# In-products of two FFNs and of a short convolution by one level of Strassen, down-products in a phase of their own

## The chip, the cores and the metric

One core of one Trainium2 chip. The metric is the device time of the whole program in microseconds: 2456.89 us, median of 3 runs (2454.88 to 2457.57).

## The reference, cut to what matters

Two layers on 1024 tokens of width 1024 (plus 256 context tokens in the first). The change touches what follows the attention and recurrence mixer of layer 0: an FFN, the short convolution mixer of layer 1, and the FFN of layer 1. FFN_HIDDEN is 2816; everything is float32.

```python
def swiglu(h, w_gu, w_down):
    gt, up = jnp.split(h @ w_gu, 2, axis=-1)
    return (jax.nn.silu(gt) * up) @ w_down

def short_conv_mixer(h, w_in, w_conv, w_out):
    bg, cg, xv = jnp.split(h @ w_in, 3, axis=-1)
    return (bg * dwconv(cg * xv, w_conv, SC_PAD)) @ w_out
...
    h = h + g1 * y            # y: the mixer of the layer
    h = h + g2 * swiglu(modulate(rmsnorm(h, norm2_g[l]), sh2, sc2), ffn_w_gu[l], ffn_w_down[l])
...
return rmsnorm(h, final_g)
```

## The kernel before, in words

**Layout.** Features lie on the 128 partitions, tokens along the row: h is [128, 8, 1024]. A float32 product is made of three fp32r matmuls of 128x512 (`product`, L795): high weight by high token, low weight by high token, high weight by low token. So each operand is first split into a high part (rounded to fp32r) and a low part (the rest), for weights by GpSimd (`split`, L622: L628 high, L631 low), for tokens by ScalarE (high) and VectorE (low).

**Memory.** The tensors made by `keep` (L114 to L140) lie at the front of each partition's memory in the order in which they are made: act_hi 0 to 32 KB, act_lo 32 to 64, w_hi4 64 to 80, w_lo4 80 to 96, raw, small ones. `at(kb, ...)` (L85) places a tensor at kb kilobytes behind what is kept at that moment, and lets others overlap it: the calls ahead of `act_hi` therefore lie over the kept tensors themselves (x_rms over act_hi), and those from L143 on lie behind all kept ones (h, w_hi2 at 32, hid_hi and z_hi at 64, o_hi at 68 and 81, o_lo at 91).

**Stages.** (1) norms, projections, gates and recurrence; (2) attention; (3) its output projection (`project_out`, 16 groups of 24 matmuls); (4) FFN 0: 11 rounds over 256 hidden columns each. A round is `gate_up` (L1109) for two tiles and two halves of 512 tokens (8 groups of 8 x 3 matmuls), then 16 down groups of 2 x 3 matmuls (half, output tile m), each added into h by VectorE (`update`, L1683). (5) Short convolution: 4 rounds of 12 groups of 24, a width-3 convolution along the tokens on VectorE (`short_conv`, L2089: L2094, L2096), then 16 down groups. (6) FFN 1 as FFN 0. (7) the final norm: transposes, squares, scaled rows, stores. During the first six rounds of FFN 0 VectorE also sums the modulation vectors of layer 1 (`mod_unit`, L1691: 6 vectors of 8 units of 128x1024).

**Order.** Every engine runs its own written-out list in order and waits on semaphores. SP issues nearly all loads in order: a weight unit of 512 KB into one of two raw buffers when the unit two before is split (`load_unit`, L405). TensorE's results go through 8 PSUM banks. The last round of a stage is arranged so that the half-0 norm of the next stage is made while half-1 groups run (`last_norms`, L1326 on ScalarE, L1743 on VectorE; `norm_sum` and `norm_spread` on TensorE, L814 and L821). A norm: squares (ScalarE), sums (VectorE), a sum over partitions (TensorE), root (ScalarE), inverse and diagonal (VectorE), spread (TensorE), scale (VectorE, L1665), shift (ScalarE, L1309, an Identity with bias), low part (VectorE).

## Time and profile before

| what | value |
|---|---|
| median of 3 runs | 2456.89 us (2454.88 to 2457.57) |
| profiled execution, span from first to last instruction | 2456.4 us; no other time of this execution is recorded, and the span lies within the runs |
| granted TensorE clock over the span | 0.996 |
| TensorE matmul busy | 2413.7 us (98%), 11158 matmuls |
| VectorE, GpSimd, ScalarE busy | 1115.1 (45%), 1053.0 (43%), 512.9 us (21%) |
| DMA | 207.08 MB, mean 84 GB/s |

Busy time is the union of the spans of an engine's instructions. A matmul's span (390 ns) overlaps that of the next, so what one costs is read from start to start. Idle time of an engine that isn't the bottleneck costs nothing.

### The profile page before, as it was taken

How to read it: one execution, taken by the hardware profiler on the slowest of the kernel's cores; microseconds unless marked ns; L12 is line 12 of the kernel's file. 1: busy time of each engine (PE TensorE's matmuls, PEld its weight loads, DVE VectorE, ACT ScalarE, POOL GpSimd, SP SyncE). 2: the span in 40 equal slices, each digit the busy share in tenths (PEclk: the TensorE clock that was granted, in tenths of full speed). 3: DMA queues.
4: the chain of work that ended last, by engine and by line, in shares of the span. 5: the costliest groups of instructions: out<-in, count | busy, mean ns of one | idle time of the engine just before them, and what ended most of it. 6: DMA issues, size and time to landing. Idle time of an engine off the chain costs nothing.

```text
span 2456.4 us, 29288 instructions
## 1 busy us (share of the span) xinstructions
PE 2413.7 (98%) x11158; PEld 1981.8 (81%) x11158; DVE 1115.1 (45%) x1427; ACT 512.9 (21%) x816; POOL 1053.0 (43%) x507
## 2 busy tenths in 40 slices
PE   8999999989999999999999999999999999999998
PEld 3888878878888888888888888887888888888887
DVE  5677858853734444422224634246522222222224
ACT  4544438851200000000002200002200000000003
POOL 3333347888633334443343243443444433333440
PEclk9999999999999999999999999999999999999999
DMA  9444465523432333211111111111211111111111
GB/s 304 155 145 156 152 164 106 105 104 104 128 116 98 104 120 120 86 43 43 51 51 37 42 44 51 51 52 43 61 52 51 43 44 48 45 43 51 51 43 69
DMA packets 223343, 207.08 MB, mean 84 GB/s; under 512 B 40135, under 2 KB 193443, under 8 KB 222755
## 3 DMA queue, kind: packets, MB, share of 16 engines
q1 hardware_dynamic: 216787, 187.16, 26.0%
q10 hardware_dynamic: 5904, 16.78, 2.0%
q0 software_dynamic: 576, 2.10, 0.2%
q8 instruction: 51, 0.84, 0.1%
q14 instruction: 25, 0.20, 0.0%
HBM read 185.73 MB, written 20.28 MB: 84 GB/s over the span
## 4 chain that ended last, share of the span: by engine, by line
PE 93%; DVE 3%; ACT 1%; issue 1%; POOL 0%; DMA 0%; SPq 0%; DVEq 0%; POOLq 0%; ACTq 0%
PE bank L798 29%; PE bank L800 29%; PE bank L799 29%; PE bank L911 1%; DVE probs L1978 1%; PE bank L1041 1%; PE bank L1067 1%; PE bank L1066 1%; PE bank L1028 1%; PE bank L832 1%; ACT probs L1504 1%; PE bank L1029 1%; DMA mod_ring<-in_mod_w 0%; DVE bank L1649 0%; DVE bank L1665 0%
## 5 line engine op out<-in xcount | busy, mean ns | idle before, releaser
L628 POOL TENSOR_TENSOR w_hi<-raw,ones 128x1024 fp32r<-128x1024 f32 x184 | 359.1, 1952 | 1176.4 <-PE bank L800 1123.0
L798 PE MATMUL bank<-act_hi,w_hi 128*128 128x512 f32 x2160 | 843.2, 390 | 2.7 <-DVE act_lo L1844 2.7
L799 PE MATMUL bank<-act_hi,w_lo 128*128 128x512 f32 x2168 | 845.5, 390 | 0.0
L800 PE MATMUL bank<-act_lo,w_hi 128*128 128x512 f32 x2160 | 841.9, 390 | 0.0
L798 PEld LDWEIGHTS bank<-act_hi,w_hi 128*128 128x128 f32 x2160 | 406.1, 188 | 87.1 <-issue 2.8
L799 PEld LDWEIGHTS bank<-act_hi,w_lo 128*128 128x128 f32 x2168 | 408.2, 188 | 84.5
L631 POOL TENSOR_TENSOR w_lo<-raw,w_hi 128x1024 fp32r<-128x1024 f32 x184 | 469.3, 2550 | 14.4
L800 PEld LDWEIGHTS bank<-act_lo,w_hi 128*128 128x128 f32 x2160 | 406.0, 188 | 85.1
L1688 DVE SCALAR_TENSOR_TENSOR h<-bank,mods,h 128x512 f32<-128x512 f32 x432 | 318.9, 748 | 243.5 <-PE bank L800 242.8
L2028 DVE TENSOR_TENSOR hid_f<-silu_g,bank 128x512 f32<-128x512 f32 x86 | 59.1, 687 | 677.9 <-PE bank L800 675.6
L798 PE MATMUL bank<-hid_hi,w_hi 128*128 128x512 f32 x704 | 275.9, 392 | 0.8 <-DVE hid_lo L2035 0.8
L799 PE MATMUL bank<-hid_hi,w_lo 128*128 128x512 f32 x704 | 274.3, 390 | 0.0
L800 PE MATMUL bank<-hid_lo,w_hi 128*128 128x512 f32 x704 | 274.3, 390 | 0.0
L1564 ACT ACTIVATE silu_g<-bank 128x512 f32<-128x512 f32 x88 | 52.6, 598 | 774.9 <-PE bank L800 774.9
L798 PEld LDWEIGHTS bank<-hid_hi,w_hi 128*128 128x128 f32 x704 | 132.2, 188 | 30.8 <-DVE h L1688 2.1
L800 PEld LDWEIGHTS bank<-hid_lo,w_hi 128*128 128x128 f32 x704 | 132.2, 188 | 28.0
L799 PEld LDWEIGHTS bank<-hid_hi,w_lo 128*128 128x128 f32 x704 | 132.2, 188 | 27.1
L1570 ACT CAST hid_hi<-hid_f 128x512 fp32r<-128x512 f32 x86 | 53.4, 621 | 460.7 <-DVE hid_f L2028 460.7
L2035 DVE TENSOR_TENSOR hid_lo<-hid_f,hid_hi 128x512 fp32r<-128x512 f32 x86 | 78.5, 913 | 59.1 <-ACT hid_hi L1570 59.1
L1699 DVE SCALAR_TENSOR_TENSOR mod_acc_f<-mod_in_f,cond,mod_acc_f 128x1024 f32<-128x1024 f32 x42 | 65.3, 1556 | 13.8 <-DMA mod_in_f<-in_mod_w 13.2
L2086 DVE TENSOR_TENSOR t_pad<-cg_sb,bank 128x512 f32<-128x512 f32 x16 | 11.0, 690 | 129.3 <-PE bank L800 129.2
L1504 ACT ACTIVATE probs<-probs,low_all 128x768 f32<-128x768 f32 (+1 forms) x64 | 63.5, 993 | 26.6 <-DVE low_all L1978 26.1
(232 smaller groups left out, 2331.0 us busy)
## 6 DMA issues: line engine op xcount, KB each, us to landing
raw<-in_ffn_w_gu SPq DMA_DIRECT2D x88, 512.0 KB, 3.8
mod_in_f<-in_mod_w SPq DMA_DIRECT2D x48, 512.0 KB, 4.5
raw<-in_ffn_w_down SPq DMA_DIRECT2D x44, 512.0 KB, 3.6
mod_in_p<-in_mod_w SPq DMA_DIRECT2D x32, 512.0 KB, 6.5
raw<-in_o_w_in SPq DMA_DIRECT2D x24, 512.0 KB, 3.7
raw<-in_e_w_in SPq DMA_DIRECT2D x20, 512.0 KB, 5.0
mod_ring<-in_mod_w SPq DMA_DIRECT2D x16, 512.0 KB, 9.0
raw<-in_e_w_out SPq DMA_DIRECT2D x16, 512.0 KB, 3.7
```

Source lines behind the costliest of these rows:

```text
L628: nc.gpsimd.tensor_tensor(w_hi, raw[:, parity, :], ones[:, 0:1].to_broadcast([P, UNIT]), ALU.mult).then_inc(s_hi, 1)
L631: nc.gpsimd.tensor_tensor(w_lo, raw[:, parity, :], w_hi, ALU.subtract).then_inc(s_split, 1)
L798: pe.matmul(dst, w_hi, x_hi, start=first, stop=False)
L799: pe.matmul(dst, w_lo, x_hi, start=False, stop=False)
L800: return pe.matmul(dst, w_hi, x_lo, start=False, stop=last)
L1504: nc.scalar.activation(probs[s % 3][:, 0:w], probs[s % 3][:, 0:w], ACT.Exp, bias=low_all[:, s:s + 1], scale=-1.0, accum_out=sums[:, s:s + ...
L1564: nc.scalar.activation(silu_g[:, q % 2, :], bank[:, b, :], ACT.Silu).then_inc(s_silu, 1)
L1570: nc.scalar.copy(hid_hi[:, tile, half * HALF:(half + 1) * HALF], from_).then_inc(s_hidh, 1)
L1688: V.scalar_tensor_tensor(out=dst, in0=bank[:, b, :], scalar=mods[:, gate, m:m + 1], in1=dst, op0=ALU.mult, op1=ALU.add).then_inc(s_hup, 1)
L1699: ins = V.scalar_tensor_tensor(out=acc[:], in0=ring[:, k % 2, :], scalar=cond[:, k, 0:1], in1=acc[:], op0=ALU.mult, op1=ALU.add)
L2028: V.tensor_tensor(hidden_from(i, q), silu_g[:, q % 2, :], bank[:, b, :], ALU.mult).then_inc(s_hidf, 1)
L2035: V.tensor_tensor(hid_lo[:, tile, sl], hidden_from(i, q), hid_hi[:, tile, sl], ALU.subtract).then_inc(s_hid, 1)
```

## The change

**In-products.** Take a pair of 128-column weight units A and B (for the FFNs gate tile and up tile; for the convolution two units of w_in), the two halves of the 8 feature tiles (k 0 to 3, k 4 to 7) and the two halves of the tokens. This 2x2x2 block product took eight half products of 4 x 3 matmuls; it is now made by seven (the Winograd form of Strassen): products 0 and 3 use plain tokens (a11, a12), products 1, 2, 4, 5 and 6 sums or the second half of the tokens, and weights or sums of weights. VectorE makes four weight sums a pair and seven combinations of the products from PSUM (U2, U3, U4, C11, C12, C21, C22). Pairs: 22 for each FFN, 12 for the convolution (8 that give c * x and are convolved, 4 "gated").

**Weight operands.** Each of the seven has one slot (128x512, high and low) that is filled when its product of the pair before is done: high part by ScalarE (before: GpSimd), low part by GpSimd. The two raw units are loaded once the low part of product 5 and of product 6 of the pair before is made.

**First products.** Products 0 and 3 of the first four pairs need only the first half of the tokens; these eight run first, while the norm and the sums of the second half are made.

**Down phase.** The gated rows z (silu x up, or gated convolution) go to DRAM (z_spill). After all pairs, chunks of 128 rows of z and of the down weight are loaded, split (ScalarE high, GpSimd low) into four slots, and multiplied two chunks a round; the last two rounds are one with four chunks.

**The rest.** The modulation sums of layer 1 run in halves of 128x512 in pairs 4 to 15 of FFN 0. All loops (Fori) are unrolled. In the diff the first seven tensors are declared ahead of act_hi, so over the kept tensors, the next six behind them. Diff, cut to its core:

```diff
+        low_f = at(32, "low_f", [P, FT, SEQ])
+        a22 = at(64, "a22", [P, 4, SEQ], F32R)
+        p1 = at(80, "p1", [P, 4, HALF])
+        silu_g = at(88, "silu_g", [P, 2, HALF])
+        mod_acc_f = at(92, "mod_acc_f", [P, UNIT])
+        conv_t = at(88, "conv_t", [P, 2, SEQ])
+        a21 = at(88, "a21", [P, 4, HALF])
...
+        a11 = at(32, "a11", [P, 2, 4, HALF], F32R)
+        a12 = at(48, "a12", [P, 2, 4, HALF], F32R)
+        slot_hi = at(64, "slot_hi", [P, 7, HALF], F32R)
+        slot_lo = at(78, "slot_lo", [P, 7, HALF], F32R)
+        t_sum = at(92, "t_sum", [P, 2, HALF])
+        t_pad = at(96, "t_pad", [P, SEQ + 2])
...
+        EARLY = 4
+        FIRST = ((0, 0), (0, 1), (3, 0), (0, 2), (3, 1), (0, 3), (3, 2), (3, 3))
+        REST = (1, 2, 4, 5, 6)
+        ACTS = {
+            0: [(a11[:, HI, k, :], a11[:, LO, k, :]) for k in range(4)],
+            1: [(act_lo[:, k, one], act_lo[:, k, two]) for k in range(4)],
+            2: [(act_lo[:, 4 + k, one], act_lo[:, 4 + k, two]) for k in range(4)],
+            3: [(a12[:, HI, k, :], a12[:, LO, k, :]) for k in range(4)],
+            4: [(act_hi[:, k, two], act_hi[:, k, one]) for k in range(4)],
+            5: [(act_hi[:, 4 + k, two], act_hi[:, 4 + k, one]) for k in range(4)],
+            6: [(a22[:, k // 2, k % 2 * HALF:(k % 2 + 1) * HALF], a22[:, 2 + k // 2, k % 2 * HALF:(k % 2 + 1) * HALF]) for k in range(4)],
+        }
...
@@ SP @@
+            def load_pair(st, p, b):
+                if p:
+                    sp.wait_ge(s_wlo, product_at(st, 5 if b else 6, p - 1) + 1)
...
+            def load_mod_half(h):
+                n, k, a = h // 16, h % 16 // 2, h % 2
+                if h >= 3:
+                    sp.wait_ge(s_macc, MACC + h - 2)
+                sp.dma_start(p1[:, 1 + h % 3, :], mod_w[1, n, k][:, a * HALF:(a + 1) * HALF]).then_inc(s_mp[h % 3], 16)
...
+                    if p:
+                        store_z(st, p - 1, 0)
+                    if p + 1 < PAIRS[st]:
+                        load_pair(st, p + 1, 1)
+                    if p:
+                        store_z(st, p - 1, 1)
+                    if p + 1 < PAIRS[st]:
+                        load_pair(st, p + 1, 0)
+                    if mods_here:
+                        for h in range(h0 + 3, min(h0 + 11, 16 * MODS)):
+                            load_mod_half(h)
...
+            def load_down(st, c):
+                r, last = c // 2, PAIRS[st] - 1
+                if r >= 2:
+                    sp.wait_ge(s_out, OUT[st] + 16 * (r - 1))
+                else:
+                    sp.wait_ge(s_prod, product_at(st, 5 if r else 2, last) + 1)
...
+            def load_hidden(st, c):
+                r, last = c // 2, PAIRS[st] - 1
+                if r >= 2:
+                    sp.wait_ge(s_out, OUT[st] + 16 * (r - 1))
+                else:
+                    sp.wait_ge(s_prod, product_at(st, 6 if r else 1, last) + 1)
+                stored_z(st, c)
...
@@ GpSimd @@
+            def down_low(st, c):
+                for j, (hi, lo, full) in enumerate((hid_slot(c), down_slot(c))):
+                    pool.wait_ge(s_h2, half_chunk(st, c) + j + 1)
+                    nc.gpsimd.tensor_tensor(lo, full, hi, ALU.subtract).then_inc(s_l2, 1)
...
+                operand_low(st, 4, 0)
+                operand_low(st, 5, 0)
+                for k in range(4):
+                    token_sum_low(st, 5, k)
+                operand_low(st, 6, 0)
+                for p in range(1, PAIRS[st]):
+                    for n in operands(st, p):
+                        operand_low(st, n, p)
...
@@ TensorE @@
+            def operand_product(st, n, p, bank_, ready=None):
+                at_, s = product_at(st, n, p), slot_at(n, p)
+                pe.wait_ge(s_wlo, at_ + 1)
+                for k in range(4):
+                    if ready is not None:
+                        pe.wait_ge(*ready(k))
+                    w = (slot_hi[:, s, k * P:(k + 1) * P], slot_lo[:, s, k * P:(k + 1) * P])
+                    mm = product(bank[:, bank_, :], w, *ACTS[n][k], k == 0, k == 3)
+                mm.then_inc(s_prod, 1)
...
+            def pair_products(st, p):
...
+                if every:
+                    pe.wait_ge(s_xfree, g)
+                    operand_product(st, 0, p, x_bank(p))
+                if g:
+                    pe.wait_ge(*made(g - 1, C22))
+                operand_product(st, 1, p, P5_BANK, ready.get(1))
...
+                if g:
+                    pe.wait_ge(*made(g - 1, C21))
+                operand_product(st, 2, p, P6_BANK, ready.get(2))
+                if every:
+                    pe.wait_ge(s_p1, g + 1)
+                    operand_product(st, 3, p, x_bank(p))
+                operand_product(st, 4, p, P7_BANK, ready.get(4))
+                operand_product(st, 5, p, P3_BANK, ready.get(5))
+                pe.wait_ge(*made(g, U2))
+                operand_product(st, 6, p, P4_BANK, ready.get(6))
...
+            def down_products(st):
+                last = ROUND[st] - 2
+                for r in range(last):
+                    for idx in range(16):
+                        down_group(st, r, idx, (2 * r, 2 * r + 1), DOWN_BANK[idx % 4], down_free(st, r, idx))
+                four = range(2 * last, 2 * last + 4)
+                for idx in range(8):
+                    down_group(st, last, idx, four, DOWN_BANK[idx % 4], down_free(st, last, idx))
...
@@ ScalarE, joint of two stages, from the norm of the second half on @@
+                first_product_copied(st, 0)
                 rms(n + 1)
+                first_product_copied(st, 1)
+                second_half(st, 0)
+                operand_high(st, *FIRST[7])
+                operand_high(st, 1, 0)
+                second_half(st, 1)
+                for m in (1, 2, 5):
+                    token_sum_high(st, m, 0)
+                second_half(st, 2)
+                operand_high(st, 2, 0)
+                for m in (1, 2, 5):
+                    token_sum_high(st, m, 1)
+                first_product_copied(st, 2)
+                second_half(st, 3)
+                for m in (1, 2, 5):
+                    token_sum_high(st, m, 2)
+                first_product_copied(st, 3)
...
@@ VectorE, a pair (mod_halves only in pairs 4 to 15 of FFN 0) @@
+                mod_halves(0, 2)
+                dve.wait_ge(s_prod, product_at(st, 3, p) + 1)
+                dve.wait_ge(s_p1, g + 1)
+                V.tensor_tensor(x, x, first, ALU.add).then_inc(s_made, 1)
+                dve.wait_ge(s_prod, product_at(st, 2, p) + 1)
+                V.tensor_tensor(first, p6, first, ALU.add).then_inc(s_made, 1)
...
+                    weight_sum(st, 1, ahead)
+                    weight_sum(st, 2, ahead)
+                mod_halves(2, 4)
+                dve.wait_ge(s_prod, product_at(st, 4, p) + 1)
+                V.tensor_tensor(first, p7, first, ALU.add).then_inc(s_made, 1)
...
```

Here product n of a pair is `operand_product(st, n, p, ...)`; `first` is the pair's copied product 0 in p1, `x` its X bank; s_prod counts products, s_wlo low parts of weight operands, s_out down groups, s_macc modulation halves.

## Rows read from the trace of the kernel before

**Rows 1.** The page, busy time of the engines and their share of the span

```profile
PE 2413.7 (98%) x11158; PEld 1981.8 (81%) x11158; DVE 1115.1 (45%) x1427; ACT 512.9 (21%) x816; POOL 1053.0 (43%) x507
```

**Rows 2.** Windows: us; PE, PEld, DVE, ACT, POOL busy (instructions); clock; DMA

```profile
690.00:1030.00 340.00, 340.00 (x1541) 282.05 (x1541) 142.12 (x168) 24.39 (x40) 135.27 (x60) 1.00 0.33 108
...
1300.00:1380.00 80.00, 78.61 (x359) 64.23 (x358) 44.42 (x72) 26.12 (x40) 18.69 (x9) 1.00 0.12 34
...
1660.00:1740.00 80.00, 78.44 (x357) 63.68 (x356) 54.23 (x80) 22.09 (x36) 30.59 (x14) 1.00 0.19 53
```

**Rows 3.** Waits of TensorE: total us, times, longest

```profile
PE bank L818 <- DVE sumsq L1649: 2.4, 3, 0.8
```

**Rows 4.** Timeline of TensorE, FFN 0: start us, us, what; first and last of 97

```profile
1099.65 0.39 PE L798 MATMUL bank<-act_hi,w_hi 128*128 128x512 f32 x1
...
1121.41 0.39 PE L798 MATMUL bank<-act_hi,w_hi 128*128 128x512 f32 x1
```

**Rows 5.** Timeline of VectorE, one round of FFN 0 apart

```profile
1172.68 0.69 DVE L2028 TENSOR_TENSOR hid_f<-silu_g,bank 128x512 f32<-128x512 f32 x1 [10.15 <-PE bank L800]
...
1238.03 0.69 DVE L2028 TENSOR_TENSOR hid_f<-silu_g,bank 128x512 f32<-128x512 f32 x1 [10.15 <-PE bank L800]
```

**Rows 6.** Timeline of TensorE, output projection; first and last of 16 matmuls

```profile
542.15 0.39 PE L798 MATMUL bank<-act_hi,o_hi 128*128 128x512 f32 x1
...
545.65 0.40 PE L798 MATMUL bank<-act_hi,o_hi 128*128 128x512 f32 x1
```

**Rows 7.** Timeline of VectorE, two down groups of the short convolution

```profile
1434.96 0.75 DVE L1688 SCALAR_TENSOR_TENSOR h<-bank,mods,h 128x512 f32<-128x512 f32 x1 [0.65 <-PE bank L800]
1436.36 0.75 DVE L1688 SCALAR_TENSOR_TENSOR h<-bank,mods,h 128x512 f32<-128x512 f32 x1 [0.65 <-PE bank L800]
```

**Rows 8.** Timeline of VectorE, a low part that met no GpSimd instruction

```profile
1174.06 0.69 DVE L2035 TENSOR_TENSOR hid_lo<-hid_f,hid_hi 128x512 fp32r<-128x512 f32 x1 [0.69 <-ACT hid_hi L1570]
```

**Rows 9.** Groups by form: xcount | busy us, mean ns | idle before

```profile
L631 POOL TENSOR_TENSOR w_lo<-raw,w_hi 128x1024 fp32r<-128x1024 f32 x184 | 469.3, 2550 | 14.4
...
L2035 DVE TENSOR_TENSOR hid_lo<-hid_f,hid_hi 128x512 fp32r<-128x512 f32 x86 | 78.5, 913 | 59.1 <-ACT hid_hi L1570 59.1
L1699 DVE SCALAR_TENSOR_TENSOR mod_acc_f<-mod_in_f,cond,mod_acc_f 128x1024 f32<-128x1024 f32 x42 | 65.3, 1556 | 13.8 <-DMA mod_in_f<-in_mod_w 13.2
...
L1570 ACT CAST hid_hi<-hid_f 128x512 fp32r<-128x512 f32 x86 | 53.4, 621 | 460.7 <-DVE hid_f L2028 460.7
...
L1309 ACT ACTIVATE act_hi<-bank,mods 128x512 fp32r<-128x512 f32 x48 | 32.8, 687 | 65.9 <-DVE bank L1665 65.7
...
L710 POOL TENSOR_TENSOR act_lo<-y_f,act_hi 64x512 fp32r<-64x512 f32 x16 | 20.5, 1283 | 16.5 <-ACT act_hi L1529 15.8
```

**Rows 10.** Timelines of VectorE and GpSimd, short convolution

```profile
1476.18 3.18 DVE L2096 SCALAR_TENSOR_TENSOR conv_t<-t_pad,par,conv_t 128x1024 f32<-128x1024 f32 x1 [0.15 <-DVE conv_t L2094]
1479.52 1.28 DVE L2096 SCALAR_TENSOR_TENSOR conv_t<-t_pad,par,conv_t 128x1024 f32<-128x1024 f32 x1 [0.15 <-DVE conv_t L2096]
...
1475.56 2.72 POOL L631 TENSOR_TENSOR w_lo<-raw,w_hi 128x1024 fp32r<-128x1024 f32 x1
```

**Rows 11.** DMA issues: xcount, KB each, median us to landing

```profile
raw<-in_ffn_w_down SPq DMA_DIRECT2D x44, 512.0 KB, 3.6
...
h<-h_spill SPq DMA_DIRECT2D x2, 1536.0 KB, 8.1
```

**Rows 12.** Timeline of ScalarE, a copy of 1024 columns

```profile
501.34 1.04 ACT L1539 CAST act_hi<-r_f 128x1024 fp32r<-128x1024 f32 x1
```

**Rows 13.** Windows around TensorE's longest gap; columns as in rows 2

```profile
531.20:534.40 3.20, 0.25 (x3) 0.10 (x1) 0.69 (x1) 0.58 (x1) 3.00 (x2) 1.00 0.60 172
534.40:541.20 6.80, 6.15 (x15) 4.80 (x16) 0.00 (x0) 0.62 (x1) 5.77 (x5) 0.50 0.27 77
```

**Rows 14.** Timeline of TensorE, sum and spread of a norm, end of FFN 0

```profile
1339.82 1.05 PE L818 MATMUL bank<-ones,sumsq 128*128 128x1 f32 x8 [0.78 <-DVE sumsq L1649]
...
1342.90 1.05 PE L825 MATMUL bank<-diag,ones 128*128 128x128 f32 x8
```

More of the change, by code:

```diff
@@ L218, in w_slot @@
         def w_slot(s):
-            return (w_hi4[:, s, :], w_lo4[:, s, :]) if s < 4 else (w_hi2[:, s - 4, :], w_lo2[:, s - 4, :])
+            return w_hi4[:, s, :], w_lo4[:, s, :]
         def out_slot(j):
@@ new lines, in x_bank, with p1_at, made, round_use @@
+        def x_bank(p):
+            return X_BANK[p] if p < EARLY else X_BANK[0]
+        def p1_at(p):
+            return p1[:, p if p < EARLY else 0, :]
+        C11, U2, U4, U3, C22, C12, C21 = range(1, 8)
+        def made(g, what):
+            return s_made, 7 * g + what
+        def round_use(st, r):
+            before = sum(len(range(r % 2, ROUND[k], 2)) for k in range(st))
+            return 32 * (before + r // 2 + 1)
+        def half_chunk(st, c):
+            return 4 * sum(ROUND[:st]) + 2 * c
@@ L1313, in norm_pair, with joint @@
+            def joint(st):
+                n, n0 = NORM[st], LAST_OUT[st]
+                if st != F0:
+                    for e in range(7):
+                        operand_high(st, *FIRST[e])
                 for f in range(FT):
```

1111 lines of the change are left out of this document (561 added, 550 removed).

## The prediction, made before the change was run

> **What bounds the kernel now.** I read the shares of the engines first: TensorE is busy in 98% of the span, no other engine in half of it [rows 1]. Then the stretches: from 690 to 1030 us TensorE is busy in all 340 us, and only the places where one stage hands over to the next show gaps, 1.4 and 1.6 us [rows 2]; its longest wait on the norms comes to 2.4 us in three waits [rows 3]. So the three stages that the change rewrites (FFN 0, short convolution, FFN 1) last as long as their matmuls do. Third, what a matmul costs: 96 steps from one 128x512 matmul to the next take 21.76 us, 0.2267 us each, although each row shows 0.39, since they overlap [rows 4]. An FFN round of 288 repeats after 65.35 us, 0.2269 each: changing groups costs nothing [rows 5].
>
> The step is not the same everywhere. Where the weights lie in o_hi and o_lo, 15 steps take 3.50 us, 0.2333 each [rows 6]; the short convolution's down groups of six take 1.40 us, again 0.2333 [rows 7]. Read with the allocation: in the fast rows weights and moving operand both lie among the kept tensors (act_hi, act_lo, w_hi4, w_lo4, the first 96 KB), or, for FFN down-products, both behind them (hid_hi, w_hi2). In both slow cases one lies in front and the other behind. I take that for the rule here.
>
> **The change part by part.**
>
> *Removed matmuls.* An in-product pair now (two column units, two token halves) is 2 x 2 x 8 x 3 = 96 matmuls; afterwards 7 x 4 x 3 = 84. There are 22 + 12 + 22 = 56 pairs: 672 fewer, at 0.2267: **-152.3 us**. The down-products keep their number.
>
> *Where the operands lie.* The new weight operands (slot_hi, slot_lo) lie behind the kept tensors. Products 0 and 3 move a11 and a12, also behind: fast. Products 1, 2, 4, 5, 6 move act_lo, act_hi and a22, all in front: slow. 56 x 5 x 12 = 3360 matmuls x 0.0067 = **+22.4**. The new down phase has both in front: fast, which gives back the three slow rounds of the short convolution, 288 x 0.0067 = **-1.9**. Bounds: no slow step at all (-22), all in-products slow (+9).
>
> *The steady pair* (from the fifth on) takes TensorE 24 x 0.2267 + 60 x 0.2333 = 19.4 us. DVE: 13 operations of which six read SBUF twice, 0.69 each where nothing blocks [rows 8] and about 0.6 from start to start: 9.3 with the gaps. GpSimd: seven low parts of 512 columns, 1.3 each (the 512-column row has 1.28 [rows 9]): 9.1. ScalarE: eight copies at 0.62 and two silus: 6. All are hidden. The tightest waits of TensorE: on C21 of the pair before, ready 0.8 us after that pair's end and wanted 5.5 after it; on the X bank, freed near 16 and wanted at 19.4. The weight loads of a pair are released by the low part of product 6, about 3.6 us into the pair before, and take 3.8; wanted at 13. Cost: 0.
>
> *The modulation sums* move into 12 pairs of FFN 0 as eight half units each, 0.65 per half (half of the unblocked 1.28 of conv_t, the same kind of step [rows 10]). DVE has 14.6 us of work there, in which 14 operations read SBUF twice and can meet GpSimd. That meeting has a price: a conv_t step that starts while GpSimd is at w_lo takes 3.18 us, the next one, alone, 1.28 [rows 10]; it waited for the whole instruction. On average it is less: hid_lo takes 0.913 [rows 9] for 0.69 alone [rows 8], so 0.22; mod_acc_f 1.556 for 1.28, 0.28. With 0.25 each: 14.6 + 3.5 = 18.1, and about 1 us for halves still landing (ring of three, each load issued on SP only when DVE has used the third before it, with z stores and weight loads queued behind these waits): 19.1 of 19.4. Just hidden; I take **+3** for all twelve, bounds 0 and 40.
>
> *The last down round of each stage.* The last two rounds become one over four chunks, so its first group needs all four. But the slots of the last two chunks are those of the round before, and their loads wait on SP for that round's end (s_out). From there: three loads of 512 KB are in after 5.7 us, four after 6.7 (one takes 3.6, 3 MB 8.1 [rows 11]: 1.8 us per further MB), the high copy 1.04 [rows 12], then four GpSimd low parts of 1024 columns at 2.55, one after the other: 9.3, 11.9, 14.4, 17.0. TensorE does nine of the group's twelve matmuls meanwhile (2.0) and stands otherwise. A gap of 3.9 us did more than cost itself: the granted clock fell to 0.50 (1.2 GHz) 3.2 us after the last matmul and stayed there for 6.8 us [rows 13]; of the loss of 3.4 I take 2.7. So 17.0 - 2.0 + 2.7 = 17.7 us, three times: **+53**, bounds 45 and 63. In other rounds the same chain of 17.0 has the 21.8 us of a round: hidden.
>
> *The joints.* Before the second half's operands exist TensorE has eight first products (21.8 us). ScalarE then has, after the spread of the norm (7.4 us in: two products, sum 0.9, spread 1.1; from the sum's start to the spread's 3.1 [rows 14]) and one scale (0.75), twelve Identity steps at 0.69 and fourteen copies at 0.62 before the fourth first product leaves its bank: at 25.1, while TensorE wants it at 21.0. 4.1, with gaps 4.5. Next, the loads of pair 1 wait for the low part of product 6 of pair 0, behind nine GpSimd instructions (11.7): issued 37.4, landed 41.2, summed, copied and split 43.9 to 45; TensorE comes at 41.8: about 3. Sum near 8 a joint, x 3 = **+24**, bounds 12 and 45, less the gaps of today's joints, 1.5 each [rows 2]: **-4.4**.
>
> *The start of the down phase.* Chunks 0 and 1 load when products 1 and 2 of the last pair are done; four low parts in a row end about 2 us after the last product. x 3: **+6**, bounds 0 and 18. *The first four pairs of the short convolution* have 14.0 us each for 9.3 + 3 conv_t steps (4.6 with their meetings): short by a little: **+3**, bounds 0 and 8. *z to DRAM and back*: stores of 0.5 MB a pair, loads long after; 0. *Unrolled instead of loops*: the attention and projection stages are unrolled already and keep 0.227 a step; 0, bounds -2 and 10. The tail has the same transposes and rows: 0, plus or minus 2.
>
> Sum: -152.3 + 22.4 - 1.9 + 3 + 53 + 24 - 4.4 + 6 + 3 = -47 us. The profiled execution has a span of 2456.4 us, 0.5 below the median of the runs (2456.9), so the two are one: **2410 us**.
>
> *A rule beside the rows.* The rows show two matmul steps by where the operands lie [rows 4, 6, 7]. The Trainium skill says otherwise (SBUF, Who interferes with whom: TensorE and ScalarE never wait on anyone; only the port pair of VectorE and GpSimd contends); by it every step would be 0.2267. Rows 6 and 7 speak against it for this case.
>
> **The rivals.**
> 1. *One matmul step for all.* The slow steps come from something else in those stretches and don't follow the operands. Without the 22.4: 2388 us. For it: the addresses stand in no row. Against: o_hi and w_hi rows 4 us apart, with the same moving operand, differ. Chance 0.14.
> 2. *The last rounds' operands are in time*, or the joints are covered better than I count: without the 53, 2357 us. Against: the wait is written in load_hidden and load_down. 0.07.
> 3. *Many small waits*: in-order queues (SP behind DVE's half units; ScalarE copying weights behind silus) cost 0.5 us in each of the 56 pairs: +28, 2438 us. For it: seven single-buffered operand slots and one raw pair. Against: several us of slack in each wait that I followed. 0.15.
> 4. *VectorE becomes the bound: slower.* Place: the 12 modulation pairs and the sum pairs of the short convolution, where it meets GpSimd. Price: with w us of wait per twice-reading operation, 12 x (14.6 + 14 w - 19.4); at w = 0.64 this eats the 47 us, and at 0.8 it gives 77, and the eight later sum pairs 7 more: 2491 us. For it: rows 10, and GpSimd never pauses long now. Against: 0.22 and 0.28 on average, and GpSimd's pieces are half as long. 0.10. The Trainium skill has this rule (SBUF, Two separate sides: of a VectorE operation with two SBUF inputs and a GpSimd one, the second to start blocks fully), and by the rule, the trace agrees in rows 10; it would give w up to 1.3 us and some 2610 us.
> 5. *The products are not fewer*: excluded by the counts in the code; 0.01.
>
> **How the numbers follow.** The forecast, 2395 to 2430, gets 0.53. A measurement of this kernel can tell about 0.2% (4.9 us) from no change. Faster: the forecast, rivals 1 and 2, and 0.13 of 3: 0.87; same 0.02 (the top of 3); slower 0.11 (4 and 5). The range takes in rival 1 below and 3 above: 2378 to 2450 us, and leaves out rivals 2 and 4.
>
> **What would show it.** Right: 4704 in-product matmuls; steps of 0.2333 in products 1, 2, 4, 5, 6 and 0.2267 in 0, 3 and the down phase; three gaps of TensorE near 10 and 4 us, ended by GpSimd's low parts, with the clock at 0.50 after them; gaps of 2 to 3 us ended by ScalarE's copies in the joints; pairs 19.4 us apart. Wrong: modulation pairs longer than 20 us with TensorE waiting for VectorE (rival 4), gaps inside every pair (rival 3), or no gap before the last round.

## The result, and the profile after

| kernel | median of the runs, us | against before, 95% interval |
|---|---|---|
| before | 2457.1 (2454.9 to 2457.6) | |
| changed | 2516.3 (2514.7 to 2518.1) | 1.0242 [1.0227, 1.0256] |

The change makes the kernel slower by 59 us; the forecast was 47 us faster. The forecast of 2410 misses by 106 us, and the measurement lies 66 us above the range.

The page of the changed kernel, busy time of the engines and the granted clock in forty slices, to be read beside [rows 1]:

```profile
PE 2351.8 (94%) x10486; PEld 1897.2 (75%) x10486; DVE 1553.6 (62%) x1963; ACT 840.4 (33%) x1327; POOL 1271.6 (51%) x735
...
PEclk9999999999998889899998999998999999999999
```

TensorE executes 672 matmuls fewer, as counted, but is busy only 62 us less instead of 152, and the span holds 162 us in which it is idle (43 before). Part of the busy time went into steps at half clock: of the 6 slices (62.8 us each) below 9, 4 lie between 750 and 1070 us, where the modulation sums run. The waits of TensorE from 535 us on (total us, times, longest); before there were 2.4 us on the norms [rows 3]:

```profile
PE bank L990 <- POOL act_lo L951: 37.6, 7, 11.5
PE bank L1025 <- DVE mod_acc_f L1833: 26.1, 6, 4.4
PE bank L990 <- ACT silu_g L1468: 16.0, 8, 3.2
PE bank L990 <- POOL act_hi L951: 14.8, 2, 11.8
PE bank L990 <- DVE act_hi L1896: 11.9, 6, 3.3
PE bank L990 <- ACT p L1460: 6.8, 3, 2.3
PE bank L990 <- DVE t_pad L1993: 6.8, 2, 6.5
```

The first and fourth line (52 us) are the last down rounds and the starts of the down phases, the fifth and sixth the joints (a joint is the change from one stage to the next): foreseen. The second is a wait that no step of the prediction has: `mod_totals` (L1025), 16 short matmuls of 128x1 that add a finished modulation sum over the partitions, stands in TensorE's order behind product 1 of every second modulation pair and waits for the last halves of the pair before. The windows (columns as in [rows 2]) place the loss: the modulation pairs, a steady stretch of FFN 1, one of the six half-clock stretches behind the totals, and the last round of FFN 0:

```profile
756.00:1062.00 306.00, 266.80 (x1052) 214.44 (x1051) 205.64 (x247) 69.16 (x120) 134.30 (x84) 0.88 0.43 131
1900.00:2200.00 300.00, 300.00 (x1293) 242.12 (x1292) 155.28 (x202) 91.32 (x157) 169.97 (x110) 1.00 0.26 80
771.40:778.20 6.80, 6.58 (x24) 5.91 (x25) 1.05 (x3) 0.00 (x0) 0.00 (x0) 0.50 0.73 228
1358.50:1375.60 17.10, 6.92 (x16) 4.96 (x17) 0.75 (x1) 8.25 (x12) 14.62 (x9) 0.50 0.30 92
```

The steady stretch is as predicted: no wait, 1293 matmuls in 300 us, 84 in 19.5 us. Of the 1052 matmuls of the first row 96 are the short ones of the totals; the other 956 would take 222 us at the steady rate, and the row lasts 306. So 84 us were lost there.

They were not lost in every pair. VectorE's first combination of a pair (L1966) dates the pairs: the twelve from 727.3 to 1047.2 us take 319.9 us, and stretches of 19.5 us (the first 21.0) take turns with six of 32.8 to 34.0 us that hold the totals. Three such dates, and the windows of the two stretches between them, each with eight halves:

```profile
782.34 0.70 DVE L1966 TENSOR_TENSOR bank<-bank,p 128x512 f32<-128x512 f32 x1 [6.16 <-PE bank L992]
801.86 0.70 DVE L1966 TENSOR_TENSOR bank<-bank,p 128x512 f32<-128x512 f32 x1 [1.19 <-PE bank L992]
835.77 0.70 DVE L1966 TENSOR_TENSOR bank<-bank,p 128x512 f32<-128x512 f32 x1 [7.08 <-PE bank L992]
```

```profile
782.30:801.90 19.60, 19.60 (x87) 15.79 (x85) 17.71 (x23) 5.14 (x9) 10.29 (x7) 1.00 0.32 95
801.90:835.80 33.90, 27.37 (x101) 21.96 (x100) 18.13 (x22) 6.37 (x11) 12.60 (x8) 0.80 0.52 163
```

In the first VectorE does all of a pair's work: it is busy for 17.7 us, or 18.0 with the gaps between its instructions, waits 0.4 us for a half load and 1.2 us for TensorE, and TensorE never waits. In the second it has the same work, 18.1 us, and the stretch is 14 us longer. So VectorE's work fits into a pair; something else makes the long stretches.

Two chains make them. VectorE's timeline in the second modulation pair (start us, us):

```profile
768.56 0.68 DVE L2006 TENSOR_TENSOR silu_g<-silu_g,t_pad 128x512 f32<-128x512 f32 x1
769.16 2.40 DVE L1833 SCALAR_TENSOR_TENSOR mod_acc_f<-p,cond,mod_acc_f 128x512 f32<-128x512 f32 x2
775.30 0.88 DVE L1830 TENSOR_SCALAR mod_acc_f<-p,cond 128x512 f32<-128x512 f32 x2 [3.74 <-PE bank L1025]
```

The last two halves of a sum stand behind everything else of their pair and end at 771.6; TensorE has waited 4.36 us for them; then VectorE waits 3.74 us for the totals, since the next sum uses the same accumulator. And SP, in order:

```profile
775.82 23.41 SPq L674 DMA_DIRECT2D p<-in_mod_w  x8
799.28 0.43 SPq L666 DMA_DIRECT2D z_spill<-silu_g  x1
799.75 0.43 SPq L657 DMA_DIRECT2D raw<-in_ffn_w_gu  x1
```

Eight half loads, each waiting for VectorE to use an earlier half, hold SP for 23.4 us; only then the next pair's raw weights are asked for. VectorE waits 22.4 us in all for raw weights in these pairs (763 to 1033 us), the weight sums and ScalarE's copies are late, and TensorE waits for `silu_first` behind those copies (the third line of its waits).

### The profile page after: what moved, and what is told of

It is laid out like the page before. It is cut to its first block, busy times and chain, and to the rows that moved or that the text cites. A ratio compares the mean times of both kernels' runs of the same rounds, so it can differ in the third digit from the quotient of the medians.

```text
span 2513.4 us, 27746 instructions
## 1 busy us (share of the span) xinstructions
PE 2351.8 (94%) x10486; PEld 1897.2 (75%) x10486; DVE 1553.6 (62%) x1963; ACT 840.4 (33%) x1327; POOL 1271.6 (51%) x735
## 4 chain that ended last, share of the span: by engine, by line
PE 70%; DVE 14%; DMA 5%; POOL 4%; issue 3%; ACT 2%; SPq 1%; DVEq 0%; POOLq 0%; ACTq 0%
PE bank L990 21%; PE bank L992 21%; PE bank L991 21%; DVE mod_acc_f L1833 3%; DMA raw<-in_ffn_w_gu 3%; POOL slot_lo L934 2%; POOL act_lo L951 2%; PE bank L1071 1%; PE bank L1025 1%; DVE probs L2238 1%; PE bank L1201 1%; DVE raw L1865 1%; DVE x_rms L1887 1%; PE bank L1227 1%; PE bank L1226 1%
## 5 line engine op out<-in xcount | busy, mean ns | idle before, releaser
L934 POOL TENSOR_TENSOR slot_lo<-raw,slot_hi 128x512 fp32r<-128x512 f32 x256 | 402.6, 1593 | 351.5 <-ACT slot_hi L1453 351.2
L990 PE MATMUL bank<-a,slot_hi 128*128 128x512 f32 x672 | 273.4, 407 | 29.6 <-ACT silu_g L1468 16.0
L992 PE MATMUL bank<-a,slot_hi 128*128 128x512 f32 x672 | 270.2, 402 | 0.0
L991 PE MATMUL bank<-a,slot_lo 128*128 128x512 f32 x672 | 269.4, 401 | 0.0
L934 POOL TENSOR_TENSOR slot_lo<-t_sum,slot_hi 128x512 fp32r<-128x512 f32 x112 | 178.3, 1612 | 160.7 <-ACT slot_hi L1453 160.7
L990 PE MATMUL bank<-act_lo 128*128 128x512 f32 x448 | 179.4, 401 | 37.6 <-POOL act_lo L951 37.6
L1966 DVE TENSOR_TENSOR bank<-bank,p 128x512 f32<-128x512 f32 x56 | 39.1, 697 | 264.7 <-PE bank L992 258.0
L990 PE MATMUL bank<-act_hi,slot_hi 128*128 128x512 f32 x448 | 182.1, 406 | 12.1 <-DVE act_hi L1896 11.9
L990 PE MATMUL bank<-act_lo,slot_hi 128*128 128x512 f32 x448 | 185.3, 414 | 3.8 <-DVE t_pad L1980 2.6
L991 PE MATMUL bank<-act_lo,slot_lo 128*128 128x512 f32 x448 | 181.6, 405 | 0.0
L992 PE MATMUL bank<-act_lo,slot_hi 128*128 128x512 f32 x448 | 181.2, 405 | 0.0
L992 PE MATMUL bank<-act_hi,slot_hi 128*128 128x512 f32 x448 | 179.9, 402 | 0.0
L991 PE MATMUL bank<-act_hi,slot_lo 128*128 128x512 f32 x448 | 179.6, 401 | 0.0
L990 PEld LDWEIGHTS bank<-a,slot_hi 128*128 128x128 f32 x672 | 130.0, 193 | 64.9 <-ACT silu_g L1468 19.5
L991 PE MATMUL bank<-act_lo 128*128 128x512 f32 x448 | 177.6, 397 | 0.0
L992 PE MATMUL bank<-act_lo 128*128 128x512 f32 x448 | 177.6, 396 | 0.0
L992 PEld LDWEIGHTS bank<-a,slot_hi 128*128 128x128 f32 x672 | 130.0, 193 | 31.4
```

The source lines that it names most:

```text
L934: nc.gpsimd.tensor_tensor(slot_lo[:, s, :], from_, slot_hi[:, s, :], ALU.subtract).then_inc(s_wlo, 1)
L990: pe.matmul(dst, w_hi, x_hi, start=first, stop=False)
L991: pe.matmul(dst, w_lo, x_hi, start=False, stop=False)
L992: return pe.matmul(dst, w_hi, x_lo, start=False, stop=last)
L1966: V.tensor_tensor(x, x, first, ALU.add).then_inc(s_made, 1)
```

## The experiments

All are timed beside the kernel before, and compared here with the changed kernel's 2516.3 us.

**1. No sums.** No half loads, no halves, no totals:

```diff
-                    mod_set(LT + mods_summed(st, p), MODS + mods_summed(st, p))
+                    V.tensor_copy(mods[:, MODS + mods_summed(st, p), :], mod_bias[:, MODS + mods_summed(st, p), :]).then_inc(s_mset, 1)
```

> The modulation sums of the second layer are left out (their 96 loads, 96 VectorE halves and 6 totals; the six rows are set to their bias alone), so the output is another. If the loss of the pairs from 756 to 1062 us is all due to these sums (43.9 us of gaps over 0.7 us and 31.7 us of steps at half clock in that stretch of the changed kernel), the time falls from 2516 by 70 to 80 us, to about 2441, and those twelve pairs take 19.5 us each as in the second FFN. If the longer gaps come from the pairs' own sums and copies, less than 20 us go.

Measured 2425.1 us (2424.2 to 2426.5). 91 us go. The stretch 760 to 1060 now holds 1292 matmuls in 300 us at full clock, like FFN 1, and the twelve pairs take 234 us instead of 320. But not all of the 91 is loss: the kernel before has the same six totals, at full clock and without a wait, and the prediction had them in its base. One of them there:

```profile
688.74 1.84 PE L832 MATMUL bank<-ones,mod_acc_f 128*128 128x1 f32 x16
690.44 0.49 PE L798 MATMUL bank<-hid_hi,w_hi 128*128 128x512 f32 x1
```

That is 1.7 us from start to start, 10 us for six. So about 81 us are the price of the sums' new place, and 78 of the 106 us of the miss lie in the term that had +3. With the sums in it and nothing else mended, the changed kernel can by this estimate come down to about 2435 us.

**2. The halves without their loads.** SP loads no half; VectorE adds what lies there.

```diff
-                dve.wait_ge(s_mp[h % 3], 16 * (2 * LT + h // 3 + 1))
+                dve.wait_ge(s_silu1, EARLY)
```

> The 96 half loads are left out, the 96 VectorE halves stay and add what lies in their buffers (another output). Theory A (two waits in a fixed order: TensorE's totals wait for the last halves of the pair before; the raw loads wait on SP behind the half loads): the totals' six gaps of 4.7 us stay with the clock after them, the six gaps at silu_first (2.2 to 3.6 us) and their clock go: 25 to 35 us less, about 2486. Theory B (VectorE is the bound through its own work and its meetings with GpSimd, rival 4 of the prediction): its work is unchanged, the time stays within 8 us of 2516.

Measured 2474.6 (2470.4 to 2478.8), 42 us less: more than theory A gave. The totals' wait stayed (18.2 us in six), that for silu_first went. 49 us of the 91 remain without any load, and the pairs' dates show where: stretches of 19.5 us, each with eight halves, take turns with six of 26.3 to 28.2 that hold the totals, 8.1 us more each on average, 49 in all. One of them on TensorE:

```profile
813.68 3.10 PE L1021 MATMUL bank<-ones,mod_acc_f 128*128 128x1 f32 x16 [3.01 <-DVE mod_acc_f L1829]
816.65 0.77 PE L986 MATMUL bank<-act_lo,slot_hi 128*128 128x512 f32 x1
```

The wait is 3.0 us, the totals take 3.0 at half clock, and ten steps behind them lose 2.1: 8.1 together. So nothing in this run is a price of VectorE's work, which was unchanged: theory B falls, and the 49 us are the totals' wait, the clock it costs, and the totals themselves (10).

**3. The sum ready earlier.**

```diff
-                mod_halves(0, 2)
+                parts = ((0, 3, 6, 8, 8) if (p - EARLY) % 2 else (0, 0, 2, 5, 8))
+                mod_halves(parts[0], parts[1])
...
-                mod_halves(6, 8)
+                mod_halves(parts[3], parts[4])
```

> Only VectorE's order is changed: the 16 halves of a sum are done earlier within their two pairs (none at the start of the first pair, none at the end of the second), so that the sum is ready before TensorE comes to its totals. Loads and amount of work are the same. Theory A: six gaps of 4.7 us (28 us) go with the half clock behind them (15 to 20 us): 40 to 48 us less, about 2472. Theory B: VectorE does the same work beside the same GpSimd work, so the gaps move and less than 10 us go.

Measured 2486.3 (2484.4 to 2490.2): 30 us, between the two. The totals' wait is gone and that for silu_first grew from 13.1 to 21.5 us in these pairs:

```profile
PE bank L990 <- ACT silu_g L1468: 21.5, 6, 3.8
PE bank L990 <- DVE p L2000: 5.7, 6, 2.3
PE bank L990 <- DVE t_pad L1981: 2.9, 5, 0.6
```

**4. The raw weights first on SP.** In a pair's entry of `products_loads`:

```diff
                         load_pair(st, p + 1, 1)
+                    if mods_here:
+                        for h in range(h0, h0 + 2):
+                            load_mod_half(h)
...
-                        for h in range(h0 + 3, min(h0 + 11, 16 * MODS)):
+                        for h in range(h0 + 2, h0 + 8):
```

> Only SP's order is changed: a pair's halves are loaded behind the next pair's raw weights, no longer three halves ahead of them. Theory A: the raw weights land some 4 us earlier, VectorE's weight sums and ScalarE's copies no longer wait for them, the six gaps of 2.2 to 3.6 us at silu_first (17 us) and the clock behind them (10 to 15 us) go: 25 to 32 us less, about 2488; if the first halves of a pair now land late, the totals' wait grows and takes some of it back. Theory B: less than 8 us go.

Measured 2489.8 (2487.6 to 2489.9): 27 us. The wait for silu_first is gone, the totals' wait is 24.9 us and up to 5.2.

**5. Both.** The edits of runs 3 and 4 together.

> Both reorderings of the runs before at once: VectorE's halves early in their two pairs, and SP loads a pair's halves behind the raw weights. Theory A (two separate waits, each uncovered when the other goes): alone they gave 30 and 27 us because the other wait grew; together they give more than the sum of the two, 57 us, up to the 91 us that leaving the sums out gave: 2516 less 60 to 80, about 2448. Theory B (VectorE's own load in these pairs, 190 us busy of 270 in the run without loads, is a floor of its own): no more than 45 us in all, about 2472.

Measured 2478.8 (2477.3 to 2482.8): 38 us, less than the sum, and within theory B's bound of 45. The forecast by theory A (60 to 80 us) misses. Both waits are gone, and these came (TensorE, the same pairs):

```profile
PE bank L991 <- DVE p L1970: 11.0, 6, 2.9
PE bank L991 <- DVE p L2001: 10.4, 6, 2.5
PE bank L991 <- DVE t_pad L1982: 4.8, 5, 1.2
```

TensorE now waits for VectorE's sums of products themselves, for two reasons. The first line is one of loads. What VectorE waits for in these pairs, one case on VectorE, and TensorE behind it:

```profile
DVE mod_acc_f L1834 <- DMA p<-in_mod_w: 29.2, 14, 4.6
```

```profile
899.98 0.75 DVE L1834 SCALAR_TENSOR_TENSOR mod_acc_f<-p,cond,mod_acc_f 128x512 f32<-128x512 f32 x1 [3.21 <-DMA p<-in_mod_w]
900.65 0.69 DVE L1968 TENSOR_TENSOR bank<-bank,p 128x512 f32<-128x512 f32 x1
901.25 0.68 DVE L1970 TENSOR_TENSOR p<-bank,p 128x512 f32<-128x512 f32 x1
```

```profile
901.99 0.50 PE L991 MATMUL bank<-a,slot_hi 128*128 128x512 f32 x1 [2.38 <-DVE p L1970]
```

The order of run 3 puts three halves at the end of a pair and three at the head of the next, six in a row, while the ring holds three and every load waits until the third half before it is used. VectorE stands 29.2 us for half loads (2.1 in the changed kernel), with the sums that TensorE needs behind them.

The second line is one of VectorE's work. In the first pair of each two, five halves stand ahead of product 5's combination (L2001), two in 2.95 us and three in 3.12, for 0.65 each alone, and VectorE is busy for 18.9 of 19.8 us:

```profile
872.90:892.70 19.80, 18.48 (x80) 14.59 (x79) 18.90 (x22) 5.76 (x10) 10.56 (x7) 1.00 0.49 146
```

That is the price of rival 4, in this order: some 10 us by the second line. In the changed kernel it is not there. By the rival's formula VectorE is over a pair of 19.4 us from w = 0.34 us on, w being the meeting with GpSimd per operation that reads SBUF twice. The stretch from 782.34 to 801.86 us shown above has 18.0 us of work, gaps included, so w = 0.24, as good as the 0.25 taken; here it is 19.2 us and 0.33. The group of the halves in the changed kernel, 1.12 us on average for 0.75 alone (the row at 899.98; neighbours overlap by about 0.1 us):

```profile
L1833 DVE SCALAR_TENSOR_TENSOR mod_acc_f<-p,cond,mod_acc_f 128x512 f32<-128x512 f32 x84 | 90.8, 1121 | 2.1 <-DMA p<-in_mod_w 2.1
```

**6. The sums spread.** SP order as in run 4, and (the totals and sets of the last two sums stand behind group 3 of rounds 4 and 8):

```diff
-        MOD_PAIRS = range(EARLY, EARLY + 2 * MODS)
+        MOD_PAIRS = range(EARLY, EARLY + 16)
...
-                halves = range(8 * (p - EARLY), 8 * (p - EARLY) + 8) if st == F0 and p in MOD_PAIRS else ()
+                halves = range(4 * (p - EARLY), 4 * (p - EARLY) + 4) if st == F0 and p in MOD_PAIRS else ()
...
+                        if st == F0 and r < 8 and idx % 3 == 0 and 3 <= idx < 15:
+                            mod_half(64 + 4 * r + idx // 3 - 1)
```

> The same sums, spread: four halves to a pair over sixteen pairs, the last two sums (32 halves) beside the first eight down rounds, totals behind product 1 and behind a down group. Theory A and B both: VectorE has about 3.5 us of halves in a pair of 19.5 us, no wait of TensorE is left, and the time is that of the kernel without the sums, 2425, within 5 us (2422 to 2432). If the half loads in the down rounds (1 MB more in 21.8 us) delay the hidden rows or weights, a gap per round appears and it is 2440 or more.

Measured 2487.6 (2484.3 to 2490.3), 60 us above the forecast. Totals waited again (10.0 us in four), since the last half still stood at a pair's end, and in the down rounds VectorE waited for half loads asked for too late, 17.3 and 11.0 us, with TensorE behind it:

```profile
DVE mod_acc_f L1842 <- DMA p<-in_mod_w: 17.3, 6, 3.6
DVE mod_acc_f L1839 <- DMA p<-in_mod_w: 11.0, 2, 9.2
```

**7. Spread, and both orders mended.** On VectorE, and on SP three half loads ahead (the edit against run 6, in part):

```diff
-                mod_halves(2, 3)
+                mod_halves(2, 4)
...
-                mod_halves(3, 4)
...
-                        for h in range(60 + 2 * c, 64 + 2 * c):
+                        for h in range(63 + 2 * c, min(67 + 2 * c, 96)):
```

> As the spread before, but a pair's four halves lie ahead of product 5's sums, so that a finished sum never lies at the end of a pair, and in the down rounds three half loads are always ahead of VectorE. Theory A (the loss was order, not VectorE's load): the four waits for totals (10 us), VectorE's waits for half loads in the down rounds (12 us) and the half clock behind them go, and the time is that of the kernel without the sums, 2425 to 2432. Theory B (VectorE's load beside GpSimd's): waits of TensorE for VectorE's products' sums remain in the pairs, 2450 or more.

Measured 2451.1 (2448.0 to 2452.8), ratio 0.9977 [0.9967, 0.9987]: 65 of the 91 us, just at theory B's bound. In the pairs TensorE's waits for the totals are gone and 4.9 us in eight waits for VectorE's `p` stay. This run changes the order and the number of halves in a pair (four for eight) together, so it doesn't tell the two apart; for the changed kernel run 2 and the windows do. Of the 26 us by which it stands above run 1, 10 are the six totals' own matmuls, now without a wait, 5 the waits for `p`, and by the pairs' dates another 5 fall into the down rounds of FFN 0. Some 6 us are not placed, and whether the waits for `p` are meetings with GpSimd or a matter of order no run tells.

**8. The last round by chunks.** Seven groups begin with chunks one and two in seven banks, then chunk three for all, then four:

```diff
+                for idx in range(7):
+                    for j in (0, 1):
+                        down_part(idx, four[j], LAST_BANK[idx], j == 0, False)
+                for j in (2, 3):
+                    pe.wait_ge(s_l2, half_chunk(st, four[j]) + 2)
+                    for idx in range(7):
+                        mm = down_part(idx, four[j], LAST_BANK[idx], False, j == 3)
```

> The merged last round of each stage starts with its first two chunks for seven output groups in seven banks (9.5 us of matmuls), then chunk three for all seven, then chunk four. The gaps of 11.9 and 3.6 us at groups 0 go to about 2.5 and 0: 13 us less for each of three stages, 39, and with the clock behind them about 46: 2516 to 2470. Rival: the norm of the first half now comes some 5 us later and the joint's gaps (2.7 and 3.7 us) grow by that: only 25 to 30 us less, 2488.

Measured 2480.9 (2479.2 to 2481.2), 35 us less. The wait of 11.5 us in FFN 0's last round is 2.6, that of 3.0 is gone; the joint's gaps grew a little (a new wait for the norm's sum, 0.7). The price of the last rounds is shown.

**9. Runs 6 and 8 together.**

> The spread sums and the split last rounds together. They lie in different stretches, so the gains add: 91 and 46 us less would be 2379, with the rival's smaller gain of the last rounds 2397. Both are below the kernel before (2457).

Measured 2449.8 (2445.3 to 2457.1), 67 us less than the changed kernel; 29 and 35 alone: they add. (The forecast of 2379 to 2397 took 91 for run 6, and misses with it.)

**10. The joints' order.** ScalarE's copies of first products 2 and 3 earlier, product 5 of pair 0 ahead of 4, and

```diff
-                    pe.wait_ge(s_xfree, g)
+                    pe.wait_ge(s_xfree, g - 3 if p == EARLY else g)
```

> Order only, in the three joints: ScalarE copies the first products 2 and 3 three items earlier; product 5 of pair 0 goes ahead of product 4, whose tokens VectorE splits last; product 0 of pair 4 waits for pair 0's bank alone, not for pairs 1 to 3 as well. Expected: the gaps of 2.7, 3.7 and 1.1 us go in each of three stages (22 us), and those at pair 4's product 0 (1.7, 6.9 and 2.0 us), with 15 to 25 us of half clock behind them: 2516 to 2458, range 2450 to 2475. Rival: VectorE and GpSimd are the pace of the joint, so the waits move to the next product: less than 20 us go.

Measured 2513.5 (2510.8 to 2515.0): 3 us, for 58 expected. It is the rival. In FFN 0's joint the waits of 2.3 and 3.3 us became many:

```profile
PE bank L990 <- POOL act_hi L946: 3.5, 4, 1.4
PE bank L990 <- DVE p L1968: 2.2, 1, 2.2
PE bank L990 <- POOL act_lo L946: 1.5, 1, 1.5
PE bank L990 <- ACT p L1460: 1.5, 2, 0.8
```

**11. All together** (runs 7, 8 and 10, and the first four groups of a down phase by chunks).

> All together: sums spread as in e_spread2, split last rounds, the joints' order, and the first four groups of a stage's first down round by chunk (2.7 us of cover for the second chunk). From 2450 of the run with spread sums and split last rounds: 20 to 40 us for the totals' and half loads' waits with their clock, 35 to 50 for the joints, 8 for the first rounds: 2365, range 2350 to 2400, which is faster than the kernel before by 2.3 to 4.3%.

Measured 2405.8 (2402.2 to 2406.9), ratio 0.979 [0.9777, 0.9804]: 2.1% faster than the kernel before, and 6 us above the range expected.

**12. Where the operands lie.** Matmuls alone, 100 combinations of places.

> No part of the kernel is computed: the matmuls of one shape (128x128 weights, 512 fp32r columns, the same three products) with weights and tokens at ten places of SBUF each, 2 to 195 KB from its start, no other engine at work. If the step depends on whether weights and tokens lie on the same side, it is 226.7 ns where both are below some 104 KB or both above some 138 KB and 233.3 ns across. If the slower step comes from the engines that write the slots meanwhile, all 100 combinations take 226.7 ns. If it comes from the weights' address alone, all tokens give the same step for one weight place.

All combinations took 226.7 ns. The prediction's rule (in front of or behind the kept tensors) is wrong, though the slow step stands in the kernel: 300 us hold 1293 matmuls, 232 ns.

**13. Where they start.** The same with offsets of 0, 4, 16, 20 and 32 bytes past a multiple of 1024.

> No part of the kernel is computed: the matmuls of the places run again, with weights and tokens at ten places, two each at 0, 4, 16, 20 and 32 bytes past a multiple of 1024. If the step depends on the offsets of weights and tokens against each other, equal offsets take 226.7 ns and unequal ones 233 ns or so; if on one operand's own offset, the step goes with the weights' or with the tokens' place; if on neither, all take 226.7 ns and the slower step comes from something else in the kernel (other engines, other waits).

Neither case that I wrote down: it matters whether exactly one of the two is at 0. Both off by anything, equal or not: 226.7 ns (all but the place c, below). One at 0 and the other off by 4 to 32: 233.3. TensorE's timeline, first and last of twelve matmuls, tokens at 0 (x_a) and then at 20 (x_g), weights at 4 (w_d):

```profile
100.12 0.40 PE L54 MATMUL bank<-x_a,w_d 128*128 128x512 f32 x1
...
102.68 0.40 PE L56 MATMUL bank<-x_a,w_d 128*128 128x512 f32 x1
...
116.62 0.39 PE L54 MATMUL bank<-x_g,w_d 128*128 128x512 f32 x1
...
119.12 0.39 PE L56 MATMUL bank<-x_g,w_d 128*128 128x512 f32 x1
```

Eleven steps: 2.56 us and 2.50, 233 and 227 ns. (Both at 0 took 226.7 with the tokens at place b and 229 to 230 with them at place a, and tokens at the place c took 229 with any weights off 0; this I leave open.)

**14. Twelve bytes.** `keep("to_64_bytes", [P, 3])` behind the last kept tensor: the later tensors then start at 109696 bytes, a multiple of 64 and of 128, not at 109684.

> The changed kernel with one unused tensor of 12 bytes kept at the end, so that all tensors behind it start at a multiple of 64 bytes. If the offset makes the slower step, the step of the steady pairs goes from 232.4 to 226.7 ns; 4704 matmuls of the pairs' products by 5.7 ns are 27 us, of which those in the twelve pairs that wait for VectorE (some 1000 matmuls, 6 us) give nothing: about 2495. If not: 2516 and 232.4 ns as before.

Measured 2501.5 (2497.9 to 2503.8), 15 us less. The step is 226.7 ns in the steady pairs (300 us of FFN 1):

```profile
1880.00:2180.00 300.00, 300.00 (x1325) 248.51 (x1324) 166.09 (x209) 93.05 (x160) 170.63 (x111) 1.00 0.27 85
```

1325 matmuls where 1293 were. The rest of the 27 us expected from the shorter step does not reach the end; TensorE's wait for silu_first grew from 16.0 to 19.8 us.

**15 and 16. The kernel of run 11 with the twelve bytes, and the same with product 4 ahead of 5 again.**

> The reordered kernel (2406) with the same 12 bytes. If the offset makes the slower step: 15 to 27 us less, about 2384, as far as TensorE and not VectorE or GpSimd is the pace; some short waits of 1 us grow. If not: 2406.

> As the run before (the reordered kernel with 12 bytes), but product 4 of pair 0 again ahead of product 5. In the joint runs the swap took away a gap of 3.7 us and its half clock (3.4 us more) and put six gaps of 1 to 2.6 us, 9 us in all, in its place: without the swap 3 gaps of 3.7 us with half clock come back and the short ones go: within 8 us of the run before, by this sum 2 us faster per stage.

Measured 2393.0 (2390.6 to 2398.8), ratio 0.9748 [0.9734, 0.9761], and 2391.3 (2389.9 to 2393.1), ratio 0.9736 [0.9723, 0.975]. The swap of products gives nothing. The last is the fastest of all, 125 us below the change as made. Its modulation pairs and a steady stretch:

```profile
763.00:1033.00 270.00, 260.54 (x1158) 212.29 (x1157) 197.84 (x230) 76.87 (x135) 145.77 (x94) 1.00 0.40 128
...
1810.00:2110.00 300.00, 300.00 (x1325) 248.51 (x1324) 164.93 (x208) 93.13 (x160) 170.30 (x111) 1.00 0.27 84
```

**17. The kernel before with the twelve bytes.**

> The kernel before, with the same 12 unused bytes ahead of its later tensors. Only the short convolution's down products (some 375 matmuls at 232.3 ns) and the first output groups mix kept and later tensors: 375 by 5.6 ns is 2 us, and 2000 matmuls of the down groups at 227.4 may give 1 us: 2454, within 2 us. If it falls by more than 6 us, part of what the aligned changed kernels gained is not the change's.

Measured 2453.1 (2451.1 to 2453.9), ratio 0.9987 [0.9978, 0.9996]: 3 us, so nearly all of what runs 15 and 16 gain is the change's once its order is mended.

## Why the prediction was wrong

By its own steps:

- *Removed matmuls* (-152): right in number.
- *Where the operands lie* (+22.4): right in size (1293 matmuls in 300 us, where 19.4 us a pair gives 1299; the twelve bytes bring 1325), wrong in cause. It is the start addresses, not the side of memory. A cause read off three stretches of one layout gave the right sum by luck of the layout, and hid that 12 bytes take it away. Rival 1 was wrong too: there are two steps.
- *The steady pair* (0): right; TensorE is busy for 300 of 300 us in FFN 1. GpSimd's seven low parts took 1.6 us each for the 1.3 taken (170 us in 300, some 11 a pair), and stay hidden.
- *The modulation sums* (+3, bounds 0 and 40): **the step that failed**: they cost about 81 us (91 by run 1, less the 10 of the totals' own matmuls). The sum of VectorE's work was right: 18.1 us without landings, and the stretch of pair 6 shows 18.0. What failed is the step from there to "just hidden": the sum was made for a pair as a whole, and nobody asked when in the pair the halves end and what TensorE has queued behind `mod_totals`, nor when SP reaches the raw loads behind eight waiting half loads, though the prediction names that queue. The totals' wait with its clock is 49 us by run 2 (10 of them the totals); runs 3 and 4, which mend one chain each, give 30 and 27 us, together 38, because the two new orders together starve VectorE of half loads and crowd its work ahead of product 5's combination.
- *Rival 4* had this place and a chance of 0.10. Its sign (modulation pairs longer than 20 us, TensorE waiting for VectorE) came: the pairs take 26.7 us on average. Its mechanism did not: it needs w above 0.34, and w is 0.24; only run 5's order brings it near (0.33), for some 10 us. The sign was too weak, since late halves give it as well as long ones. And where it gives "some 2610" for w = 1.3, its formula has 12 x (14.6 + 18.2 - 19.4) = 161 us, so about 2570 before the pairs of the short convolution.
- *The last rounds* (+53): right. (By its own slope of 1.8 us per MB the loads come to 5.4 and 6.3 us, not 5.7 and 6.7; that changes nothing.) The waits are 11.5 and 3.0 us in FFN 0 and 11.8 and 3.0 in the short convolution; the first lies within a stretch of 17.1 us at half clock. Run 8 took 35 us back.
- *The start of the down phase* (+6): three waits of 1.8, 2.9 and 4.2 us, 8.9 in all, within its bounds.
- *The joints* (+24): too small. FFN 0's waits of 2.3 and 3.3 us are of the size foreseen, but each was followed by 3.4 to 6.8 us at half clock, for which this term had nothing, and the 3.3 us wait is for VectorE's token splits (L1896), which the step did not have. From these numbers I estimate 11 us a joint, 33 in all. *The first pairs of the short convolution* (+3): 6.5 us and half clock, a wait for banks of pairs 1 to 3 that product 0 of pair 4 does not need.
- *The clock* was priced once, behind the last rounds; each of the six waits for the totals (4.4 us) brought 6.8 to 10.2 us of it at half. It is part of the 81 us. In the window of run 11's first joint shown at the end no gap reaches 2 us, and the clock stays up.
- *The rule of the Trainium skill* (SBUF, Who interferes with whom: TensorE never waits on anyone) was weighed against rows 6 and 7. Run 12 agrees with it for plain places, and runs 13 and 14 show that the slower step needs no other engine either: nothing else was at work in run 13. So the rows did not speak against the rule, and I was wrong to say so. *The other rule of the Trainium skill* (SBUF, Two separate sides: of a VectorE operation with two SBUF inputs and a GpSimd one that reads SBUF, the second to start blocks fully) has its trace here: single halves of up to 1.79 us where most take 0.75, and 1.12 on average.

What stays open: what run 5's order would give with the half loads further ahead; how much of the waits for `p` in run 7 is meetings with GpSimd; and the steps of run 13 with both operands at 0.

## What to carry to other kernels

A sum of an engine's work over a period shows that it can fit, not that it does: for every instruction that another engine waits for, write down at which moment of the period it ends, and what stands behind its waiter, and for every in-order queue which later load a waiting one holds back. Put work that fills gaps early in its period and spread it over all periods, and price a wait of TensorE with the half clock that it brings: in the modulation pairs waits of 1.8 to 4.4 us brought 3.4 to 10.2 us of it. A sign of being wrong must fit one mechanism only: "TensorE waits for VectorE" fits both too much work and work in the wrong place, and VectorE's busy share of a pair tells them apart. And look at start addresses: a tensor of 12 bytes gave 13 to 15 us in the changed kernels, and 3 in the kernel before.

## What was not expected of the hardware

- The step of 128x512 fp32r matmuls is 226.7 ns or 233.3 ns, by whether exactly one of weights and tokens starts at a multiple of 1024 bytes (run 13) and the other 4 to 32 bytes off one. In the kernel a multiple of 128 was enough (run 14).
- A row of short waits left the granted clock at full where fewer, longer ones did not. The window from 639 to 664 us of run 11 (a joint with eight gaps from one matmul to the next of 1.1 to 1.9 us), and of run 7 (three gaps, of 2.7, 3.7 and 1.1 us):

```profile
639.00:664.00 25.00, 17.78 (x70) 12.06 (x69) 24.65 (x19) 12.60 (x23) 23.04 (x14) 1.00 0.01 3
```

```profile
639.00:664.00 25.00, 18.73 (x67) 13.73 (x66) 24.65 (x20) 13.51 (x25) 23.08 (x14) 0.88 0.07 21
```

TensorE is busy for less time in the first, and yet does more matmuls, since the clock is 1.00 and not 0.88.
